# A fused two-block layer on one core: x loaded first, the opening's norms on two engines, conditioning columns and transposes placed later than their products

## What is computed

```python
def _rmsnorm(x, g):
    xf = xf * lax.rsqrt(jnp.mean(xf * xf, axis=-1, keepdims=True) + NORM_EPS)
def _modulate(x, g, shift, scale):
    return _rmsnorm(x, g) * (1 + scale) + shift
def _ada(cvec, w_ada, b_ada):                      # w_ada: 1024 x 6144
    mod = jax.nn.silu(cvec) @ w_ada + b_ada        # six chunks of 1024
# x: 512 x 1024, ctx: 256 x 1024
h  = _modulate(x,   n_pre_mix, sh1,  sc1)          # chunks 0 and 1 of mod
hc = _modulate(ctx, n_pre_mix, csh1, csc1)
q, k, v, z, xbc, dt_raw, gates = _split_in(h @ w_in)   # w_in: 1024 x 10304
xbc = silu(depthwise_conv5(xbc))                   # 2048 x columns, 512 B, 512 C
# scan over chunks of 128 rows, 32 heads in 4 groups, forward and backward
u = y * silu(z); u = u * rsqrt(mean(u * u over each group's 512) + eps)
```

## Time and profile before

| | us |
|---|---|
| median of 3 runs | 4026.04 (4020.71 to 4030.50) |
| profiled execution, its own time | 4025.7 |
| its span | 4023.9 |
| TensorE busy | 3660.3 (91%) |
| mean granted TensorE clock | 0.969 of full |

### The profile page before, as it was taken

How to read it: one execution, slowest core, us unless ns; L and a number is a source line. 1 busy time by engine, 2 the same in 40 slices (tenths; PEclk the granted TensorE clock), 3 DMA queues, 4 the chain that set the end, 5 groups by cost and what they waited for, 6 DMA issues and landing times.

```text
span 4023.9 us, 32988 instructions
## 1 busy us (share of the span) xinstructions
PE 3660.3 (91%) x12600; PEld 1766.6 (44%) x12600; DVE 1148.0 (29%) x2602; ACT 772.9 (19%) x1778; POOL 441.4 (11%) x397
## 2 busy tenths in 40 slices
PE   6888899899999887888888888899999999999999
PEld 3355454444444433333233334555444445554444
DVE  2345555424210220311101114543221134432211
ACT  2024444322210200000000002332110123221100
POOL 1002223302100000000000001101221011012210
PEclk8899999999999999999999998999999999999999
DMA  8322223211222479999999991102222120022220
GB/s 253 126 72 79 69 84 94 69 58 37 79 71 96 174 283 409 409 409 409 409 409 409 409 392 54 37 27 84 84 77 75 57 84 32 32 96 67 84 71 34
DMA packets 302154, 634.08 MB, mean 158 GB/s; under 512 B 32499, under 2 KB 145763, under 8 KB 301743
## 3 DMA queue, kind: packets, MB, share of 16 engines
q1 hardware_dynamic: 240480, 591.96, 39.3%
q10 hardware_dynamic: 61519, 40.02, 3.6%
HBM read 625.50 MB, written 10.24 MB: 158 GB/s over the span
## 4 chain that ended last, share of the span: by engine, by line
PE 52%; DMA 19%; DVE 3%; ACT 1%; issue 1%; POOL 0%; SPq 0%; DVEq 0%; ACTq 0%
PE psum L307 26%; DMA arena<-in_w_exp_up_dram 7%; DMA arena<-in_w_exp_gate_dram 7%; PE psum L1572 6%; DMA arena<-in_w_exp_down_dram 4%; PE psum L2851 4%; PE psum L2815 4%; PE psum L2357 3%; PE psum L1396 2%; PE psum L2836 1%; PE psum L1424 1%; PE psum L2306 1%; PE psum L1405 1%; PE psum L2275 1%; PE psum L2750 1%
## 5 line engine op out<-in xcount | busy, mean ns | idle before, releaser
L307 PE MATMUL psum<-arena 128*128 128x512 f32 (+1 forms) x3200 | 1302.6, 565 | 7.6 <-DVE arena L1782 5.0
L307 PEld LDWEIGHTS psum<-arena 128*128 128x128 f32 x3200 | 609.8, 192 | 682.2 <-issue 653.6
L2357 PE MATMUL psum<-arena 128*64 128x512 f32 x3072 | 693.7, 596 | 153.0 <-DMA arena<-in_w_exp_up_dram 76.5
L2357 PEld LDWEIGHTS psum<-arena 128*64 128x64 f32 x3072 | 233.3, 136 | 594.6 <-issue 574.1
L1572 PE MATMUL psum<-arena 128*128 128x512 f32 x768 | 351.9, 613 | 0.0
L732 PE MATMUL psum<-arena 128*128 128x512 f32 (+1 forms) x768 | 269.8, 511 | 1.3 <-ACT arena L550 1.3
L1572 PEld LDWEIGHTS psum<-arena 128*128 128x128 f32 x768 | 147.5, 196 | 193.8 <-issue 192.9
L1504 DVE CUSTOM_DVE_ANT_0 arena<-psum,arena 128x512 f32<-128x512 f32 (+3 forms) x224 | 113.9, 546 | 387.0 <-PE psum L1396 386.8
L2894 POOL TENSOR_SCALAR arena<-arena 128x512 f32<-128x512 f32 x88 | 138.4, 1572 | 696.5 <-ACT arena L2873 696.5
L732 PEld LDWEIGHTS psum<-arena 128*128 128x128 f32 x768 | 151.0, 199 | 125.1 <-issue 114.5
L2900 DVE SCALAR_TENSOR_TENSOR arena<-arena 128x512 f32<-128x512 f32 x88 | 66.2, 753 | 426.5 <-POOL arena L2894 426.5
(11 more groups left out here) (283 smaller groups left out, 2946.7 us busy)
## 6 DMA issues: line engine op xcount, KB each, us to landing
arena<-in_w_exp_gate_dram SPq DMA_DIRECT2D x128, 1024.0 KB, 18.8
arena<-in_w_exp_up_dram SPq DMA_DIRECT2D x128, 1024.0 KB, 18.5
arena<-in_w_exp_down_dram SPq DMA_DIRECT2D x128, 1024.0 KB, 18.8
arena<-in_w_in_dram SPq DMA_DIRECT2D x64, 1024.0 KB, 5.3
arena<-in_w_up_dram SPq DMA_DIRECT2D x88, 512.0 KB, 4.8
arena<-in_w_ada_dram SPq DMA_DIRECT2D x24, 1024.0 KB, 8.5
arena<-in_w_down_dram SPq DMA_DIRECT2D x20, 1024.0 KB, 5.1
arena<-acs_scratch ACTq DMA_DIRECT2D x64, 256.0 KB, 3.7
```

The source lines that it names most:

```text
L307: mm = pe.matmul(shaped(b, l, r), l, r, start=kt == 0, stop=kt == nkt - 1)
L2357: mm = pe.matmul(banks[n][64 * j:64 * j + 64, :], lhs[:, kt, 64 * j:64 * j + 64], w, start=kt == 0, stop=kt == 2 * nkb - 1)
```

## The change

It does six things. (1) x is requested first, in four pieces, and the small vectors come on SP, first the 72 columns that the opening needs. (2) ACT squares two tiles of x and DVE the other two, DVE and ACT scale them, POOL no longer does; ACT's first guess of the root needs one trip instead of two. (3) The ada halves are taken in the order (1,0), (0,0), (1,1), (0,1), and half of HT is made after each pair. (4) In the BC stage the columns or row of half k-1 follow the product of half k. (5) In the projections `turn i-2` stands before `conv i`, where `turn i-1` stood after it; `turn 2` stands before `tb`, `turn 3` after the first tile of z. (6) ACT and DVE rearrange HT, and DVE scales the last z, before the loop of the attention begins, and POOL takes one rotation earlier.

```diff
 def pe_start(pe):
-            for i in range(6):
-                pe_turn(pe, ("vec", i), PALL, ...)
-            run(pe_ada_cols(pe, 0, r0bufs))
-            run(pe_ada_cols(pe, 1, r0bufs))
-            for nm, _, nt, xn_, _, _ in parts1:
-                pe_turned(pe, nm, nt, xn_)
+            pe_vec(pe, 0)
+            pe_ada_product(pe, 1, 0)
+            pe_ada_product(pe, 0, 0)
+            pe_ada_cols(pe, 1, 0, r0bufs[0])
+            pe_turned_x(pe, 0)
+            pe_ada_cols(pe, 0, 0, r0bufs[1])
+            pe_ada_product(pe, 1, 1)
+            pe_turned_c(pe, 0)
+            for i in range(1, 6):
+                pe_vec(pe, i)
+            pe_ada_cols(pe, 1, 1, r0bufs[0])
+            pe_turned_x(pe, 1)
+            pe_turned_c(pe, 1)
+            pe_ada_product(pe, 0, 1)
+            pe_ada_cols(pe, 0, 1, r0bufs[1])
 def pe_ada_rest(pe):
+            for k in range(9):
+                if k < 8:
+                    pe_ada_product(pe, *ADA_REST[k])
+                if 0 < k < 5:
+                    pe_ada_cols(pe, *ADA_REST[k - 1], ADB[(k - 1) % 2])
+                elif k:
+                    a = ADA_REST[k - 1]
...
+                yield
 def pe_proj(pe, g, pool):
             for i in range(4):
+                if i > 1:
+                    pe_turn_x(pe, g, i - 2, pool)
                 pe_conv(pe, ("x", g), i, pool)
-                if i:
-                    pe_turn_x(pe, g, i - 1, pool)
                 yield
+            pe_turn_x(pe, g, 2, pool)
...
-                if n == 1:
+                if n == 0:
                     pe_turn_x(pe, g, 3, pool)
 def dve_proj(dve, g):
             for i in range(4):
-                if i:
-                    dve_turn_x(dve, g, i - 1)
+                if i > 1:
+                    dve_turn_x(dve, g, i - 2)
                 dve_conv(dve, ("x", g), i, 4 * g + i)
                 yield
+            dve_turn_x(dve, g, 2)
 def dve_program(dve):
             wait_all(dve, CHUNKS_END)
+            dve_by_blocks(dve)
+            dve_scale_z(dve, 3)
```

More of the change, by code:

```diff
@@ L483, in pe_ada_product, with dve_ada_copy @@
                     mm.then_inc(*up(S("pe_ada"), ("wfree", (a, kt // 4)), ("full", a) if kt == 7 else ("half", a)))
-        def dve_ada_product(dve, a, r):
+        def dve_ada_copy(dve, chunk, half, r):
+            a = ("ada", chunk, half)
             dve.wait_ge(*at("full", a))
             dve.tensor_copy(r[0:96, :], PS.of(a)[0:96, :]).then_inc(*up(S("dve_ada"), ("free", a), ("ada_r", a)))
[L489 to L499, removed]
@@ L579, in act_start, with act_scaled @@
+        def act_scaled(act, nm, i, src, dst):
+            act.activation(dst, src, ACT.Copy, bias=0.0, scale=ssq_of[nm][0][:, i:i + 1]).then_inc(*up(S("act_xn"), ("xn", nm, i)))
+        def act_start(act):
+            for i in range(4):
+                act.dma_start(xin[:, i, :], xT[:, i, :]).then_inc(*up(S(f"x_in{i}"), ("x_in", i), by=16))
+            act.dma_start(cin, A["ctx"].rearrange("a (t p) d -> p (a t) d", p=128)).then_inc(*up(S("c_in"), ("c_in",), by=16))
             act.wait_ge(*at("col", 0))
@@ new lines, in act_start, with dve_square @@
+            for half in range(2):
+                wait_mod1(act, half)
+                for j in (4 * half + 1, 4 * half + 3):
+                    turned_x(act, act_turned, j)
+                turned_c(act, act_turned, 2 * half + 1)
+        def dve_square(dve, nm, i, src):
+            if M.count.get(id(S("dve_sq")), 0):
+                dve.wait_ge(*now(S("dve_sq")))
+            dve.tensor_tensor_reduce(out=spare, in0=src, in1=src, scale=1.0, scalar=0.0, op0=ALU.mult, op1=ALU.add,
+                                     accum_out=ssq_of[nm][0][:, i:i + 1]).then_inc(*up(S("dve_sq"), ("sq", nm, i)))
@@ L680, in pe_ada_rest @@
-            yield from pe_ada_cols(pe, 4, ADB)
-            for chunk in (2, 5):
-                for half in range(2):
-                    a = ("ada", chunk, half)
-                    pe_ada_product(pe, a)
-                    b = open_bank(pe, ("row", chunk, half), PALL)
-                    pe.wait_ge(*at("ada_r", a))
-                    pe.matmul(b[0:1, :], sel[0:96, 0:1], ADB[0][0:96, :], start=True, stop=True).then_inc(
-                        *up(S("pe_ada"), ("full", ("row", chunk, half))))
-                    yield
```

393 lines of the change are left out of this document (207 added, 186 removed).

## The result

| | before | after |
|---|---|---|
| median of 5 runs, us | 4030.50 (4020.71 to 4037.74) | 3986.86 (3983.33 to 3988.05) |
| profiled execution, its own time, us | 4025.7 | 3987.49 |
| its span, us | 4023.9 | 3985.7 |
| mean granted TensorE clock | 0.969 | 0.973 |

The ratio is 0.9891, with a 95% interval from 0.9876 to 0.9906: a gain of 43.6 us by the medians and of 38.2 by the spans of the two profiled executions. The forecast was a gain of 57.4 and 3968 us.

A forecast was written before the change was run, and what follows sets the result against it. TensorE was taken to bound the kernel, the touched stages losing idle time and lower-clock matmuls after it. Terms 15.4 + 45 + 2.5 - 18 + 12.5 = 57.4 off 4025.7 gave 3968.3 us; own range 3955 to 3982, given 3940 to 3990.

The forecast's parts named there:

- the neighbours: Cases beside the forecast, partly taken into its range: turns pay 3942 to 3923 (0.13), BC held 3989 (0.14), opening 3979 (0.05).
- the rival that the BC stage is held: BC stage: short idle spells remain or w_ada pieces come late; only 24.5 of waits won, 3989 us; chance 0.14.
- Opening: Start to first convolution tile: from 54.86 to 39.5 us, a gain of 15.4, from 9 to 19.7.
- product (1,1) ends at about 29.2 (1.4 for its second MB): Opening: half (1,1) is in at 27.7 us, its product ends 1.4 later, TensorE's remaining list follows.
- with the shift and scale hidden under the first four of eight steps of the tile: Opening, first convolution tile: shift and scale add no time; the data allow a start at 35.1 us.
- BC stage: Ada columns one product later: 116 us against 161.0, gain 45, bounds 24.5 and 47.
- the thirteen DMA issues that ACT had ahead of the stage: BC stage: now behind ACT's first silu, making ACT some 4 us late for the second tile; eight banks hide it.
- Group 0: Projection of group 0: tile 3's transposes move into an existing wait; gain 2.5, from 0 to 3.
- Chunk loops: Three loops with projections: z's first tile waits for the bank of `turn 2`, sweep 5.9 later each; loss 18.
- After the last chunk: TensorE's waits for the blocks and scaled z and slow matmuls behind them: gain 12.5, from 5 to 14.
- Behind 830 us: Stages after 830 us: no change of length forecast; any change there was named as a sign of being wrong.
- that a shift of the early program moves all that follows by as much: Whole kernel: assumed because expert loads are requested by slots that TensorE frees; no later gain or loss.

The follow-up runs named there:

- product_first: Changed kernel with the opening's product of ada half (0,1) ahead of the last 24 transposes of x and ctx: 3985.4 us, ratio 0.9886 to before.
- rpb_spread: Changed kernel with ACT's eight bias table copies issued one in each step of the BC stage: 3984.3 us, ratio 0.9881 to before.
- bc_alone: Kernel before with part 4 alone, ACT's thirteen issues staying ahead of the BC stage: 3985.3 us, ratio 0.9894 to before.
- turn3_late: Changed kernel with `turn 3` alone moved back behind the second tile of z: 3989.9 us, ratio 0.9906 to before.
- turns_back: Changed kernel with part 5 alone undone, in all four groups: 3967.7 us, ratio 0.9847 to before.
- turn2_early: Changed kernel with `turn 2` alone moved back behind `conv 3`: 3980.1 us, ratio 0.9875 to before.
- turns01: Changed kernel with `turn 2` back behind `conv 3` and `turn 3` back behind the second tile of z: 3961.5 us, ratio 0.9830 to before.
- best_back: Changed kernel with part 5 undone, bias table copies spread over BC steps, product (0,1) ahead of the opening's last transposes: 3954.6 us, ratio 0.9816 to before.
- best_mix: Changed kernel with `turn 2` and `turn 3` back in groups 1 to 3, bias copies spread, product (0,1) ahead of last transposes: 3950.2 us, ratio 0.9805 to before.
- six_undone: Changed kernel with part 6 alone undone: 3998.5 us, ratio 0.9920 to before.

## Why the prediction was right, and where it was off

The time, 3986.9, lies in the range that was given, 3940 to 3990, but 5 us above the forecast's own range (3955 to 3982) and 19 above the forecast. It is inside because the range took in the neighbours, and close to the 3989 of the rival that the BC stage is held. Of the 19 us, 14.3 are in the first two terms of the sum, and three quarters of the gain that was forecast for these two did come.

**Opening: 11.2 for 15.4.** The step that failed is "product (1,1) ends at about 29.2 (1.4 for its second MB)", which took that product as bound by data. Its data were in, but TensorE came to it only at 29.91. The data of half (0,0) let TensorE go on at 23.24; behind that stood 1.90 of product, 1.05 of columns, 1.94 of transposes, a wait of 1.02 and columns of 1.02. That makes 2.8 us at the last product (37.92, forecast 35.1). Of the other 1.4 the bank is 1.1: "with the shift and scale hidden under the first four of eight steps of the tile" looked at the data of the tile and not at its PSUM bank. The bank taken longest ago was that of the fifth transposed column of x, and DVE frees it only with that shift and scale. product_first shows it: with another set at that place in the order of banks the tile starts at 42.92, before DVE begins that shift and scale (43.30).

**BC stage: 34.9 for 45.** The mechanism held; rpb_spread took 116.6 us for the stage, against 116. What was off was the sentence on "the thirteen DMA issues that ACT had ahead of the stage": I priced them as time of ACT, and not as traffic. Behind the first silu they fall on the pieces of w_ada that the faster stage now needs. That cost 6.6 us in the profiled run (3.02 of wait and the low clock behind it; 1.9 to 6.6 in the seven profiles), and the first tile's low spell another 2.9. This was the rival "the clock or the ring holds the BC stage", which had named these copies, with half of its price (9.5 of 20.5). bc_alone shows the term without most of that: 42.5.

**Group 0: 3.7 for 2.5.** Right, and by the reason given: with `turn 3` back at its old place the projection takes 104.3 (turn3_late), close to the 104.75 of before.

**Chunk loops: -18.9 for -18.** DVE's copy of `turn 2` was forecast to start 81.0 us after `conv 0`; it starts at 80.4. z was forecast at 81.7, and starts at 81.2, 8.9 later than before (forecast 9.4). The sweep was forecast 101.7 after `conv 0`; it is 101.6. ACT's last padded copy comes 1.7 us sooner than before, forecast 1.1. turns_back gives the size by itself: 20.5. But the reason was not all of it. The forecast held the bank of `turn 2` for the one cause; turn2_early and turns01 show that with this cause gone, `turn 3` ahead of the last chunk steps costs 16.2 of the 24.4. The sum came out because the two hide each other: it needed only the one that ends last. The rule of the Trainium skill (Perfetto Trace Analysis, Optimization Strategy) that a repeating gap can mean too little PSUM fits what the trace shows, three waits on a bank, 38.7 us together. The order of the work removed them; more banks were not tried.

**After the last chunk: 10.3 for 12.5.** Right in mechanism. The lead grows by 12.0 from 743.74 on; 1.8 had been lost in the last chunk loop, which the forecast left out. No wait for the blocks is left; one of 1.77 us at the transposes of z is.

**Behind 830 us: -3.2 for 0.** The assumption "that a shift of the early program moves all that follows by as much" failed by these 3.2 us; the forecast had named a changed length there as a sign of being wrong. The work there is the same. Two traces of the same instructions, of the changed kernel and of rpb_spread:

```profile
908.06 1.09 PE L1457 MATMUL psum<-arena 128*128 128x128 f32 x8 [2.79 <-DVE arena L1577]
909.08 1.13 PE L1448 MATMUL psum<-arena 64*128 64x512 f32 x4
```

```profile
900.83 1.97 PE L1461 MATMUL psum<-arena 128*128 128x128 f32 x8 [2.79 <-DVE arena L1581]
902.73 2.08 PE L1452 MATMUL psum<-arena 64*128 64x512 f32 x4
```

The wait is 2.79 us in both. In one the clock stays up behind it (the eight transposes take 1.09), in the other it falls (1.97, and 2.08 for a product of 1.13). Of the twelve profiles, which all have this wait, two keep the clock over the four matmuls of that product and ten do not (1.65 to 2.08), the kernel before among them. From this place to 970 us the lead of rpb_spread over the changed kernel falls from 7.2 to 3.5 us, though no instruction differs. Against the kernel before, the lead at 900 us was kept to within 1 us in turns_back, best_back and best_mix and grew by 3.8 in turns01. It fell by 2.2 to 3.2 in bc_alone, the changed kernel and turn3_late, by 6.1 in six_undone, by 7.4 and 7.7 in product_first and rpb_spread, and by 10.8 in turn2_early. So in one run an early gain is passed on only to within some 11 us, and an edit worth less than that can't be priced by the end of one profile. Why the clock falls behind a given wait in one run and not in another stays open.

## What to carry to other kernels

Before a reader's copy is moved later, write down which set next takes its bank and who waits to open it: the wait that was missed in the opening and the largest loss of this change come from there, and two moves that hide each other have to be undone together to see their price. When a stage gets faster, look at all traffic that falls into it, not only at the instructions that issue it. A product put one step ahead of what uses it was worth 42.5 us in one stage (bc_alone), 22.6 of waits and 19.8 of matmuls at the low clock. The same idea in the loops, where TensorE waits for ACT in either order, gained some 1.5 us a loop by the mean of the profiles, not clear of their noise, and lost 6 where it held a bank.

## What was not expected of the hardware

The same wait of TensorE is followed by a spell at 1.2 GHz in one run and not in another: 0.88 and 1.11 us ahead of the first tile (low in four of seven), 2.79 us at 908 (low in ten of twelve). In the opening the product of half (1,1), 16 matmuls, took 2.77 us in seven profiles and 4.2 to 4.5 in three, with the same wait of 1.02 us ahead of the columns before it in all. Eight copies from HBM to HBM in rows of 1,860 bytes kept all DMA engines busy at 197 GB/s, half the rate of the weight loads.
